# Prompt attention in head pairs on halves of the TensorE array, one head's matmuls and then the other's, with the output kept feature-major on chip

## What is computed

```
scores = q_head . k_head * SCALE + mask          # per query and key
p      = exp(scores - max);  o = (p @ v) / sum(p)
o_a    = six heads of group A, three dilated windows mixed by their denominators (one softmax over weighted keys)
o_cmp, o_slc, o_win = six heads of group C over 63 compressed keys, the selected (here: all causal) blocks, a window of 512
oc     = gate[0] * o_cmp + gate[1] * o_slc + gate[2] * o_win          # gates: sigmoid of z, per head
cat    = concat(o_a [384], o_b [256, recurrence], oc [384])
x      = x + cat @ w_o
x      = x + experts(rms_norm(x))                # top 1 of 4 groups, top 2 of 4 experts
```

## Time and profile before

| | us |
|---|---|
| median of 3 runs (2540.66 to 2553.93) | 2545.53 |
| span of the profiled execution | 2535.2 |
| prompt attention, first score to last output | 1349.8 to 1804.5 |
| its tiles 0 to 3 / 4 to 7 | 186.3 / 268.4 |
| mix, first instruction of TensorE | 1835.6 |
| first expert matmul | 2068.1 |

### The profile page before, as it was taken

The page is one execution under the profiler, slowest core; times in us unless marked ns, Lnnn a source line. Parts: engine busy times, 40 slices in busy tenths (PEclk is TensorE's granted clock), DMA queues, the critical chain, the costliest instruction groups (busy, mean ns, idle before and its releaser), DMA issues. The chain is left out here.

```text
span 2535.2 us, 32455 instructions
## 1 busy us (share of the span) xinstructions
PE 2072.4 (82%) x9999; PEld 1344.6 (53%) x10000; DVE 976.3 (39%) x2516; ACT 566.6 (22%) x1292; POOL 118.7 (5%) x174
## 2 busy tenths in 40 slices
PE   7899999688566762999977999999499739999991
PEld 4454555355354552878866777877445314444440
DVE  1221222122188884044434555555233413333334
ACT  1111111211122220022214565555211101111110
POOL 0000000000000001000000000000000030000004
PEclk9999999899766655699997799999799869999996
DMA  7111111444300003322315433322333516775226
GB/s 258 50 45 39 43 50 45 150 141 160 126 11 21 21 22 51 101 67 88 88 49 168 162 113 107 103 99 91 115 101 101 190 34 232 280 260 197 89 83 228
DMA packets 180897, 277.29 MB, mean 109 GB/s; under 512 B 42284, under 2 KB 147532, under 8 KB 180284
## 3 DMA queue, kind: packets, MB, share of 16 engines
q1 hardware_dynamic: 167500, 203.59, 25.3%
q0 software_dynamic: 8704, 55.85, 6.1%
q10 hardware_dynamic: 4608, 16.78, 1.6%
HBM read 226.59 MB, written 78.95 MB: 121 GB/s over the span
## 5 line engine op out<-in xcount | busy, mean ns | idle before, releaser
L218 PE MATMUL p_acc<-p_w,p_hT 128*128 128x384 f32 (+2 forms) x1152 | 419.9, 527 | 27.2 <-DVE p_hT L276 27.2
L218 PEld LDWEIGHTS p_acc<-p_w,p_hT 128*128 128x128 f32 x1152 | 223.1, 194 | 222.5 <-issue 146.0
L2226 PE MATMUL m_hid<-m_w,m_xT 128*128 x512 | 237.0, 617 | 13.2 <-DMA m_w<-in_moe_w 10.4
L1023 PE MATMUL pa_sc<-pa_kT,pa_qT 128*128 128x512 f32 (+4 forms) x528 | 197.4, 480 | 1.1 <-ACT pa_qT L1078 1.1
L1048 PE MATMUL pa_op<-pa_v,pa_pT 128*128 128x64 f32 (+1 forms) x1452 | 196.2, 278 | 0.0
L1162 DVE CUSTOM_DVE_ANT_0 pa_p<-pa_sc,pa_mask 128x256 f32<-128x256 f32 (+7 forms) x192 | 117.3, 611 | 195.4 <-PE pa_sc L1023 116.9
L1048 PEld LDWEIGHTS pa_op<-pa_v,pa_pT 128*128 128x128 f32 (+1 forms) x1452 | 184.4, 198 | 11.2 <-issue 10.0
L2226 PEld LDWEIGHTS m_hid<-m_w,m_xT 128*128 128x128 f32 x512 | 97.8, 196 | 133.7 <-issue 133.7
L2170 PE MATMUL m_acc<-m_wo,m_catT 128*128 128x512 f32 (+1 forms) x288 | 134.8, 624 | 9.6 <-DVE m_st L2462 5.8
L1105 ACT ACTIVATE pa_p<-pa_p,pa_nb 128x256 f32<-128x256 f32 (+7 forms) x192 | 126.2, 657 | 73.1 <-DVE pa_nb L1165 72.6
L2607 DVE COPY m_xT<-m_tp 128x512 f32<-128x512 f32 x32 | 22.1, 692 | 297.3 <-PE m_tp L2218 297.3
(11 more groups left out here) (353 smaller groups left out, 2505.4 us busy)
## 6 DMA issues: line engine op xcount, KB each, us to landing
m_w<-in_moe_w SPq DMA_DIRECT2D x48, 1024.0 KB, 9.8
sa_kv<-in_cache_a SPq DMA_DIRECT2D x20, 1536.0 KB
out_a_s<-in_cache_a POOLq DMA_DIRECT2D x8, 3048.0 KB
sc_x<-in_cache_c SPq DMA_DIRECT2D x136, 128.0 KB
tmp_ys<-m_cat ACTq DMA_DIRECT2D x16, 512.0 KB, 2.9
tmp_ys<-m_x ACTq DMA_DIRECT2D x16, 512.0 KB, 3.2
p_w<-in_w_in SPq DMA_DIRECT2D x4, 1536.0 KB, 11.3
p_w<-in_w_in SPq DMA_DIRECT2D x3, 2048.0 KB, 17.1
```

The costliest lines, as they stand in the source:

```text
L218: last = pe.matmul(acc[c % 4][:, 0:cw], hT[:, k, :], w[:, k, c0:c0 + cw], start=k == 0, stop=k == KD - 1)
L1023: last = pe.matmul(sc[u % 2][:, lo:hi], qT[s][:, j, pr, :], kT[x][:, kp, k0 * C + lo:k0 * C + hi], start=True, stop=True)
L2226: last = pe.matmul(hid[s][:, :], xT[:, k, :], w13[:, bass.ds(e % WB * KD + k, 1), :].rearrange("p o n -> p (o n)"), start=k == 0, stop=k = ...
```

## The change

In `prompt_attention` the unit is now a pair of heads: 96 pairs. Chunks stop at n + 1, and the compressed job has one chunk of 64 keys. Queries are transposed once per tile for group A and once for group C, without zeros. Scores contract over 64 rows: head 0 on rows 0 to 63, head 1 on rows 64 to 127, each with PSUM banks of 512 columns of its own; keys over 512 take a second block. All blocks of head 0 are issued, then all of head 1. In `values` v is the stationary operand (64 columns) and the transposed probabilities the moving one (128 columns): head 0 writes PSUM partitions 0 to 63, head 1 partitions 64 to 127, so the output has features on partitions. All chunks of head 0 come first, then head 1's. The division by the sums, and the gates of group C, are widened over 64 features and transposed on TensorE (`weights`, `shares`); VectorE multiplies and adds into `catT`, which stays on chip (`out`). All masks and gates are loaded at the start of the stage, ahead of most keys, and TensorE waits for them; the first cache copy of GpSimd waits for nothing.

In `mix_and_experts` only the recurrence's 256 columns are loaded and transposed for a prompt tile (two transposes for eight); w_o is loaded in three pieces with the rows of group C in the order of the pairs; the old path remains for the decode tile. w_o shares SBUF with experts 1 and 2, so only expert 0 is loaded ahead and the other two after the last projection.

```diff
 prompt_attention, TensorE
-        pe.wait_ge(const_in, 16)
+        pe.wait_ge(const_in, 16 * 6)
...
-                    masked.wait(pe, i, u - 1) if u else masked.wait(pe, i - 1, U - 1)
-                    for lo in range(0, n * C, 512):
-                        hi = min(lo + 512, n * C)
-                        last = pe.matmul(sc[u % 2][:, lo:hi], qT[s][:, j, pr, :], kT[x][:, kp, k0 * C + lo:k0 * C + hi],
-                                         start=True, stop=True)
-                    last.then_inc(scored.sem, 1)
+                    for j in range(2):
+                        r = slice(HD * j, HD * j + HD)
+                        for b, (lo, hi) in enumerate(blocks[u]):
+                            B = block0[u] + b
+                            if j == 0:
+                                after(pe, masked, 2 * (B - 1))
+                            last = pe.matmul(sc[B % 2][j][:, 0:hi - lo], qT[y][n % 2][r, pr, :],
+                                             kT[ji][r, two[j][2], first * C + lo:first * C + hi], start=True, stop=True)
+                            if j:
+                                last.then_inc(scored, 1)
...
-                    for c in range(n):
-                        last = pe.matmul(op[u // NU][:, h * HD:h * HD + HD], pT[u % 2][0:C, c, :],
-                                         v[x][0:C, k0 + c, vc * HD:vc * HD + HD], start=c == 0, stop=c == n - 1)
+                    for j in range(2):
+                        vc = two[j][3]
+                        for c in range(number):
+                            last = pe.matmul(op[J % 2][HD * j:HD * j + HD, pr * P:(pr + 1) * P],
+                                             v[ji][0:C, first + c, vc * HD:vc * HD + HD],
+                                             pT[u % 2][0:C, j * number + c, :], start=c == 0, stop=c == number - 1)
                     last.then_inc(summed, 1)
...
+                def shares(u):
+                    pe.wait_ge(rec, REC * (J + 1))
+                    for pr in range(PAIRS):
+                        last = pe.transpose(tp[f % 2][:, pr, :], rw[J % 2][:, 2 * pr:2 * pr + 2, :].rearrange(
+                            "p j d -> p (j d)"), ident[:, :])
...
+                for s in range(STEPS):
+                    if s < NU:
+                        scores(s)
+                    if s in queries_at:
+                        queries(*queries_at[s])
+                    if 0 <= s - LAG < NU:
+                        transposes(s - LAG)
+                    if 0 <= s - LAG - 1 < NU:
+                        values(s - LAG - 1)
+                    if is_last(s - LAG - 2):
+                        shares(s - LAG - 2)
 SyncE and GpSimd
+                    if x == 0:
+                        sp.dma_start(mask[0][:, :], jobs[0][2](NT - 1, 0, NT)).then_inc(const_in, 16)
+                        sp.dma_start(zg[:, :, :], t["zr"][0:SEQ, Z_G:Z_W].rearrange("(n p) c -> p n c", p=P)
+                                     ).then_inc(const_in, 16)
+                        sp.dma_start(mask[1][:, :], t["mask_cmp"][:, 16:136]).then_inc(const_in, 16)
+                        sp.dma_start(mask[2][:, :], jobs[2][2](NT - 1, 0, NT)).then_inc(const_in, 16)
+                        sp.dma_start(mask[3][:, :], jobs[3][2](NT - 1, NT - 1 - CWIN // P, CWIN // P + 1)
+                                     ).then_inc(const_in, 16)
...
-                    done.wait(pool, b * IT // DEC_B, 1)
+                    after(pool, done, b * NT * UJ // DEC_B)
 VectorE
+                        for j in range(2):
+                            dve.tensor_tensor_reduce(p[u % 3][j][:, lo:hi], sc[B % 2][j][:, 0:hi - lo],
+                                                     mask[ji][:, at + lo:at + hi], 1.0, -3e38, ALU.add, ALU.max,
+                                                     mx[:, u % 3, b, j:j + 1]).then_inc(masked, 1)
...
+                        dve.tensor_tensor(part[:, :, :], src, rs[J % 2][:, :, :], ALU.mult).then_inc(done, 1)
+                        dve.wait_ge(done, J + 1)
+                        dve.tensor_tensor(dst, dst, part[:, :, :], ALU.add).then_inc(drawn, 1)
 mix_and_experts
-                    for k in range(KD):
-                        last = pe.transpose(tp[:, k, 0:T], cat[0:T, k * P:(k + 1) * P], ident[0:T, 0:T])
+                        pe.wait_ge(ob_in[i % 2], 16 * (i // 2 + 1))
+                        for k in range(2):
+                            last = pe.transpose(tp[:, k, :], ob[i % 2][:, k * P:(k + 1) * P], ident[:, :])
...
+                        cats = catT[:, k, 0:T] if T < P else allT[:, k, i * P:(i + 1) * P]
...
-                for e in range(WB):
+                load_expert(0)
+                sp.wait_ge(pe_s.sem, pe_s.at(PT, 2))
+                for e in range(1, WB):
                     load_expert(e)
```

More of the change, by code:

```diff
@@ L786, in prompt_attention @@
 def prompt_attention(nc, t, sets, jobs):
[L800 to L827, removed]
+    LAG, PAIRS, NT = 2, 3, PT
+    UA, UJ = len(jobs) * PAIRS, len(jobs)
+    sizes = [P, HD, P, P]
+    units = []
+    for n in range(NT):
+        for ji, job in enumerate(jobs):
+            first, number = job[5][n]
+            if ji == 1:
+                first, number = 0, 1
+            elif number > n + 1 - first:
+                number = n + 1 - first
+            for pr in range(PAIRS):
+                units.append((n, ji, pr, first, number))
@@ L833, in prompt_attention @@
         ident = sb("ident", [P, P])
[L834 to L839, removed]
@@ L908, in prompt_attention, with heads @@
+        def heads(u):
+            n, ji, pr, first, number = units[u]
+            of = [w for w in jobs[ji][4] if w[0] == pr]
+            return [next(w for w in of if w[1] == j) for j in range(2)]
         with nc.Block() as block:
@@ L1052, in step @@
-                def step(now, lagged, last, past):
-                    if now:
-                        if now[1] == NU - AHEAD:
-                            queries(now[0], 1)
-                        if now[1] == U - AHEAD:
-                            queries(now[0], 0)
-                        scores(*now)
-                    if lagged:
-                        transposes(*lagged)
-                    if last:
-                        values(*last)
-                run(step)
+                for n in (NK - 2, NK - 1):
+                    key_bank_read(pe, n)
@@ new lines, in _, with queries, scores @@
+                pe.wait_ge(k_ev_a, -(-NK // 2) + 2)
+                def queries(n, y):
+                    f = of_query[(n, y)]
+                    taken(pe, f - 2)
+                    pe.wait_ge(q_in[y][n % 2], 16 * (n // 2 + 1))
+                    for pr in range(PAIRS):
+                        last = pe.transpose(tp[f % 2][:, pr, :], q[y][n % 2][:, pr * P:(pr + 1) * P], ident[:, :])
+                    last.then_inc(filled, 1)
+                def scores(u):
+                    n, ji, pr, first, number = units[u]
+                    y, C = min(ji, 1), sizes[ji]
+                    if pr == 0 and n and ji < 2:
+                        taken(pe, of_query[(n, y)])
+                    two = heads(u)
+                    for j in range(2):
[8 more added lines that the diff above has]
+                                last.then_inc(scored, 1)
@@ new lines, in transposes @@
+                def transposes(u):
+                    n, ji, pr, first, number = units[u]
+                    C = sizes[ji]
+                    for f, lo, hi in of_unit[u]:
+                        taken(pe, f - 2)
+                        after(pe, exped, 2 * u + 1 + (hi > number))
+                        for i in range(lo, hi):
+                            j, c = divmod(i, number)
+                            last = pe.transpose(tp[f % 2][0:C, i - lo, :], p[u % 3][j][:, c * C:(c + 1) * C], ident[:, :])
+                        last.then_inc(filled, 1)
```

601 lines of the change are left out of this document (303 added, 298 removed).

## The result

| | before | after |
|---|---|---|
| median of four runs each, us | 2543.1 | 2478.22 |
| ratio of the runs | | 0.9736, 95% interval 0.9702 to 0.9771 |
| span of the profiled execution | 2535.2 | 2476.8 |
| prompt attention starts | 1325.8 | 1332.4 |
| from there to the first score | 24.0 | 39.5 |

A stage starts with its first instruction on any engine, and a tile ends with VectorE's last instruction for its output. The change is faster by 2.6%.

The account below looks back on a forecast made before the run. TensorE was taken to bound prompt attention. Large tiles -62, small tiles -38, start +9 and mix -5 sum to -96: span 2535.2 becomes 2439, plus 10.3 to the median gives 2450 us, range 2405 to 2510.

Parts of the forecast that it names:

- the main case: Prompt attention: three waiting instructions are passed; scores overlap wholly, values take 4c-4 steps for c chunks; 2450 us, chance 0.52.
- rival (b): Prompt attention: only one instruction passes; tiles 4 to 7 at 245 us, small ones -32; 2494 us, chance 0.10.
- Rival (a): Prompt attention: no limit, head 1 runs beside head 0 throughout, values 2c steps; -123 us, 2422, chance 0.18.
- (c): Prompt attention: program order holds, overlap only at the seam of two heads; 2522 us, chance 0.06.
- (d): Prompt attention: halves run one after the other, stepping between them pays a change of shape; 2578 us, chance 0.07.
- Rival (e): Prompt attention: TensorE's clock on half tiles stays at the 1.2 GHz level; about 2615 us, chance 0.07.
- The large tiles: Tiles 4 to 7 of prompt attention: from 268 to 206 us, -62, bounds -52 to -72.
- Both below 6.95, so they hide: Pair of eight chunks: VectorE under 5 us and ScalarE about 4 hide behind TensorE's 6.95.
- Changes of shape: Between scores, transposes and values of each pair: 288 changes at 0.11 us, +32 us, bounds 26 to 37.
- Small tiles: Tiles 0 to 3 of prompt attention: 148 us taken, between 110 and 153; -38, bounds -20 to -55.
- Start: Start of prompt attention: extra loads +4, gates +1, cache copy 0 to 11 us; +9 together, bounds +3 to +16.
- Mix: Mix stage: first transpose -3, fewer transposes and gates -3 over eight tiles; together -5, bounds -10 to +2.

Follow-up runs that it names:

- the split run: Changed kernel with TensorE issuing the first two banks of transposes, then the previous pair's values, then the other banks: 2468.7 us, ratio 0.9697.
- the run with the late copy: Changed kernel with GpSimd's first cache copy waiting again until the first job is done: 2466.1 us, ratio 0.9667.
- all four changes: Changed kernel with values in turn, transposes split around values, first cache copy late, masks and gates loaded after keys: 2422.5 us, ratio 0.9471.
- the mix's start: Kernel with all four changes, plus scores in turn and identity, first rows and w_o loaded ahead of the mix's small constants: 2389.9 us, ratio 0.9365.

## Why the prediction held, step by step

**Right.** 2478 lies in the range of 2405 to 2510, 28 us above the forecast of 2450; the profiled span fell by 58 where 96 were expected. The time alone would not have told the main case from rival (b), whose 2494 is nearer; the trains of instructions do. The mechanism on which most hung is the main case's: up to three instructions wait for a busy half and the next one, for the free half, passes. Scores overlap wholly where no wait interrupts them, a pair of eight chunks takes 28 value steps, and the price of a step is 0.109. The runs with values in turn, in groups of four and one after the other bear the count out (16, 21 and 32 steps; for the groups 20 were expected). Each matmul comes with a weight load, and no run tells whether the limit counts the one or the other. Rival (a), overlap throughout, fell with the train of 3.33 us; (b), (c) and (d) with the start of head 1 at the thirteenth. Rival (e) did not come: 0.99 in tiles 4 to 7. The Trainium skill's rule of strict program order ("TensorE: Matmul & The Clock Gate", Part 3, The mechanism) does not hold in this trace: 1728.048 precedes three starts of head 0 that the program has ahead.

**Luck in the number.** The miss by parts is larger than by the sum. The large tiles gave 24.9 us where 62 were forecast, outside the bounds of 52 to 72; small tiles and mix gave 13 more than forecast and hide that much of the 44 by which large tiles and start fell short. The 10.3 us that the forecast adds from span to median were the distance of one execution: in the changed kernel it is 1.4 (2478.2 against 2476.8), so that the span misses its forecast of 2439 by 38 us and the median by 28.

**The step that failed: "Both below 6.95, so they hide".** I compared sums of busy time per pair, VectorE under 5 us and ScalarE 4 against TensorE's 6.95. The sums were right (VectorE 136 us in tiles 4 to 7), but not their place in a round. Before, a head filled two banks, one for each copying engine, and TensorE had a whole step until it needed them again. A pair fills four, so two copies must end within one step of TensorE, behind masks that cannot start before that step's scores. I read who is busy and not who is queued behind whom, though I had named that queue for the small instructions ("behind them queue the next pair's masks"). The gaps between transposes came to 24.8 us in the large tiles, and the split run took 13 of these back by laying the copies beside values. The sign that the prediction named for this came true: VectorE and ScalarE release TensorE's waits in the large tiles (9.6 and 7.6 us).

**Changes of shape: size.** I took 0.11 for each of three, 0.33 a pair. Start to start, the first instruction after a change comes 0.203 after the last one instead of 0.109, and the second one late as well: 0.160 to 0.165 after a first transpose or value, 0.520 for 0.429 after a first score of 512 columns. That is 3 x 0.094 + 2 x 0.055 + 0.091 = 0.48 a pair, 7 us more over 48 pairs. With the second score block's wait (5 us by the run with scores in turn) the large tiles come to 206 + 25 + 7 + 5 = 243, measured 243.5. So -62 became -24.9.

**Small tiles.** -38 forecast, -45.6 measured, within the bounds; 1.39 times the floor of 110 gives 153, 140.7 was measured. Part of this is luck: four of the kernels above took 8 to 10 us more in tiles 0 and 1 by the clock (last section).

**Start.** +9 forecast with +16 as the bound, +15.5 measured: the copy 10.6 (0 to 11 allowed, some 4 taken) and the masks 5.6 (5 forecast). Only the copy was mis-sized. I took a value between the ends of what I could not see, where the row of 0.90 busy queues at 326 GB/s spoke for the upper end: at that rate 3.5 MB last 11 us (an estimate), so here the transfer cost its whole length. The first score came at 1371.9, past the 1353 to 1366 that was named, by the 6.6 us of the stages ahead.

**Mix.** -5 forecast, -10.1 measured, at the bound of -10, but from other places. The start gave nothing instead of 3: the last constant landed 30.0 us after the stage's begin for 24.5 before. That w_o comes in three pieces and the decode tile's rows now stand ahead of it is a likely reason, which no run tests; the run with the early w_o shows that the wait for these constants can be had back in part (22.4 us for 31.3). The tiles gave more than the 3: projections ran from the first to the last in 159.9 us instead of 167.7, of which 1.1 is the clock in the first tile (the same 32 instructions in 15.51 us for 16.57, at a granted clock of 0.90 for 0.84). Rows of the changed kernel, and two of the kernel before in the same place:

```profile
1787.53 0.69 PE L2186 MATMUL m_tp<-m_ident,m_ob 128*128 128x128 f32 x2 [33.09 <-DMA m_rb<-in_moe_be]
...
1823.45 0.41 PE L2186 MATMUL m_tp<-m_ident,m_ob 128*128 128x128 f32 x2
1824.68 7.13 PE L2198 MATMUL m_acc<-m_big,catT 128*128 128x512 f32 x16 [0.81 <-ACT catT L2314]
```

```profile
1874.67 1.07 PE L2160 MATMUL m_tp<-m_ident,m_cat 128*128 128x128 f32 x8
1876.71 7.13 PE L2170 MATMUL m_acc<-m_wo,m_catT 128*128 128x512 f32 x16 [0.97 <-DVE m_st L2462]
```

From the transposes to the projection 1.23 us pass; before, eight transposes and two copies took 2.04. That is 0.8 a tile, six transposes and the longer copy behind them, which I had left out.

The late loads of two experts cost nothing, as forecast: from the start of the last projection to the first expert matmul it is 62.0 us in both.

## What to carry to other kernels

Matmuls on halves of the array ran side by side only as far as the order let the second half's instruction past the first's, and three waiting ones were the most that it passed: issue them in turn (the values here), or at most four in a row per half (the scores here). When a change makes the work unit larger, count the buffers that one unit goes through and follow one buffer around its loop (who fills, who empties, what stands ahead of the emptying on that engine); busy sums do not show such waits. A background copy that is let go early can be paid in full where the foreground's loads are the bound: 10.6 us here.

## What the hardware showed beyond that

The clock of the small tiles differs between kernels whose work there is nearly the same. From 1390 to the end of tile 0, the changed kernel and the one with values in turn show in the table by stretch:

```profile
1390.00:1408.80 18.80, 17.69 (x119) 10.81 (x119) 11.17 (x58) 12.77 (x48) 0.26 (x1) 0.75 0.08 22
```

```profile
1390.00:1410.80 20.80, 20.80 (x103) 12.56 (x101) 10.46 (x52) 11.80 (x42) 0.28 (x1) 0.50 0.08 20
```

In the second, TensorE was busy for all 20.8 us and yet stayed at 0.50; tiles 0 and 1 took 73.6 us instead of 63.8, and the run with the late copy shows the same. Kernels with split transposes fall on either side (64.1 alone, 71.5 with all four changes, 62.0 with the mix's start as well). Why one rises earlier was not settled, so up to some 10 us of a comparison between these kernels can be this clock's, and tiles 4 to 7 (granted clock 0.98 to 1.00 in the four of them where it was read) are the better measure of an edit.
